# Second projection of the last feed forward by seven products instead of eight

## The reference, cut to what matters

```python
D_MODEL = 1024; SEQ = 512; D_FF_2 = 4 * D_MODEL
# end of second_block, x is [1, 512, 1024]
f = rmsnorm(h, pre_ff_g[l]) @ w_ff1[l]          # [512,1024] @ [1024,4096]
f = jnp.square(jax.nn.relu(f)) @ w_ff2[l]       # [512,4096] @ [4096,1024]
h = h + rmsnorm(f, post_ff_g[l])
```

## Time and profile before

| | before |
|---|---|
| median of 3 runs | 1729.57 us (1729.56 to 1731.13) |
| the profiled execution, own time | 1730.73 us |
| its span, first to last instruction | 1729.0 us |
| mean granted clock of TensorE | 0.998 |
| TensorE busy | 1715.3 us, 99% |
| VectorE busy | 1209.1 us, 70% |
| ScalarE busy | 820.2 us, 47% |
| feed forward of the last block, steady part | about 1440 to 1690 us |

### The profile page before, as it was taken

The page is one execution under the profiler, slowest core; times in us unless marked ns, Lnnn a source line. Parts: engine busy times, 40 slices in busy tenths (PEclk is TensorE's granted clock), DMA queues, the critical chain, the costliest instruction groups (busy, mean ns, idle before and its releaser), DMA issues.

```text
span 1729.0 us, 26320 instructions
## 1 busy us (share of the span) xinstructions
PE 1715.3 (99%) x10458; PEld 1497.2 (87%) x10458; DVE 1209.1 (70%) x1975; ACT 820.2 (47%) x1449; POOL 46.4 (3%) x103
## 2 busy tenths in 40 slices
PE   9999999999999999999999999999999999999998
PEld 8777788999999887777989999989888898999997
DVE  4588787777787735666877777868446876677776
ACT  4477744444445235664444444443565555333342
POOL 0212000000000000000000000000000000000000
PEclk9999999999999999999999999999999999999999
DMA  8343332333334232224133333352314224333331
GB/s 276 113 134 118 119 89 87 109 98 110 101 99 153 86 105 84 81 91 122 39 103 98 110 110 97 99 165 82 110 44 140 63 73 126 106 98 98 100 109 49
DMA packets 220125, 181.36 MB, mean 105 GB/s; under 512 B 9906, under 2 KB 178771, under 8 KB 220003
## 3 DMA queue, kind: packets, MB, share of 16 engines
q1 hardware_dynamic: 217954, 175.48, 33.1%
q0 software_dynamic: 2048, 4.20, 0.9%
HBM read 173.32 MB, written 7.38 MB: 105 GB/s over the span
## 4 chain that ended last, share of the span: by engine, by line
PE 93%; DVE 4%; ACT 1%; DMA 1%; issue 1%; POOL 0%; DVEq 0%; POOLq 0%
PE ps L733 29%; PE ps L734 28%; PE ps L735 28%; PE ps L1092 1%; PE ps L1137 1%; PE ps L1163 1%; PE ps L1112 1%; PE ps L1151 1%; DMA arena<-arena 1%; PE ps L987 1%; DVE wlo L1701 0%; DVE xl L1793 0%; PE ps L1102 0%; PE ps L972 0%; ACT whi L1321 0%
## 5 line engine op out<-in xcount | busy, mean ns | idle before, releaser
L1701 DVE TENSOR_TENSOR wlo<-raw,whi 128x1024 fp32r<-128x1024 f32 (+1 forms) x276 | 317.6, 1167 | 181.3 <-ACT whi L1321 181.0
L733 PE MATMUL ps<-xh,whi 128*128 128x256 f32 (+1 forms) x1016 | 332.4, 327 | 2.3 <-DVE xl L1793 2.3
L735 PE MATMUL ps<-xh,wlo 128*128 128x256 f32 (+1 forms) x1016 | 326.1, 321 | 0.0
L734 PE MATMUL ps<-xl,whi 128*128 128x256 f32 (+1 forms) x1016 | 325.9, 321 | 0.0
L1321 ACT ACTIVATE whi<-raw 128x1024 fp32r<-128x1024 f32 (+1 forms) x276 | 274.6, 1007 | 80.9 <-DMA raw<-in_w_ff 36.4
L733 PE MATMUL ps<-whi,hh 128*128 128x512 f32 x728 | 288.7, 397 | 1.4 <-DVE wlo L1701 1.3
L734 PE MATMUL ps<-wlo,hh 128*128 128x512 f32 x728 | 285.2, 392 | 0.0
L735 PE MATMUL ps<-whi,hl 128*128 128x512 f32 x728 | 283.6, 390 | 0.0
L733 PEld LDWEIGHTS ps<-xh,whi 128*128 128x128 f32 x1016 | 194.1, 191 | 25.8 <-issue 8.8
L735 PEld LDWEIGHTS ps<-xh,wlo 128*128 128x128 f32 x1016 | 194.1, 191 | 14.4
L734 PEld LDWEIGHTS ps<-xl,whi 128*128 128x128 f32 x1016 | 194.4, 191 | 12.2
(11 more groups left out here) (272 smaller groups left out, 2935.3 us busy)
## 6 DMA issues: line engine op xcount, KB each, us to landing
raw<-in_ffn_w_in SPq DMA_DIRECT2D x88, 512.0 KB, 3.8
raw<-in_w_ff SPq DMA_DIRECT2D x64, 512.0 KB, 4.2
raw<-in_ffn_w_out SPq DMA_DIRECT2D x44, 512.0 KB, 3.9
raw<-in_a_w_qkv SPq DMA_DIRECT2D x22, 512.0 KB, 5.5
raw<-in_w_in SPq DMA_DIRECT2D x20, 512.0 KB, 3.8
raw<-in_kv_w SPq DMA_DIRECT2D x16, 512.0 KB, 4.1
bias_skewed<-bias_rows SPq DMA_DIRECT2D x8, 640.0 KB
arena<-arena POOLq DMA_DIRECT2D x64, 64.0 KB, 2.7
```

The source lines that it names most:

```text
L733: e.matmul(o, ah, bh, start=start, stop=False, **more)
L734: e.matmul(o, ah, bl, start=False, stop=False, **more)
L735: return e.matmul(o, al, bh, start=False, stop=stop, **more)
L1701: e.tensor_tensor(lo[:, 0:n], src, f32(hi[:, 0:n]), ALU.subtract).then_inc(s.lo, 1)
```

## The change

Six of the eight groups (`SEVEN_FIRST` 1 to `SEVEN_LAST` 6) are computed by seven products in place of eight. A group's operand is a 2 by 2 matrix of quarters on the left (256 tokens by two hidden blocks: a11, a12, a21, a22) and on the right (two hidden blocks by 512 columns). The seven products are P1 to P7 in the order of the table `SEVEN`: a11, a12, s1, s4, s2, s3, a22. Each has two halves a and b (token tiles), and a half is six matmuls of 512 columns, as a piece was.

- **TensorE** does 14 halves a group instead of 16 pieces. 9548 instructions become 9476.
- **Left operands.** Hidden values are no longer split as they come but kept as fp32 words. VectorE forms the four sums s1, s2, s4, s3 (`left_sum`), ScalarE writes the high part of each of the seven left operands and VectorE the low part (`left`), two products ahead of use.
- **Right operands.** There are seven tiles to split a group instead of four. Four are loads of weights into buffers of `x`. Sums of weight tiles are made by four accumulating transfers a group, each 512 KB from HBM added to the buffer (GpSimd's queue): in one chain the same buffer is split, added to, split again, three times over (P1, P3, P5 and P7 use its states), and another buffer is loaded and added to once (P6).
- **Results.** P1, P2 and P7 add to the left columns: VectorE, six additions a group. P3 to P6 go to the right columns: ScalarE copies each half from PSUM to one of four slots, with its sign, and GpSimd issues a transfer that adds it to `mb` (eight a group, 256 KB each). A bank that a later product goes on adding to is first read out.
- **Order.** "2222" becomes "2212", seven halves for one pair.
- **Around it.** `x` is parked in HBM during the stage and brought back; the gain is loaded late; some semaphores are merged; and all weight tiles, in every stage of the kernel, are laid out on the host so that a tile is 128 rows of 4 KB in HBM.

Counted from P1b, one group's order on TensorE, with the first projection's products between: P2a X6 P2b P3a X4 X3 P3b P4a X5 X1 P4b X7 X2 P5a P5b X6 P6a P6b X4 X3 P7a P7b X5 X1 P1a X7 X2 P1b, 14 X and 14 halves.

```diff
-FEED_PIECES = ["1111"] + ["2222"] * 13
+FEED_PIECES = ["1111"] + ["2212"] * 13
+SEVEN_FIRST, SEVEN_LAST = 1, 6
+SEVEN = [("a11", 0, True, 0, 0, 1), ("a12", 1, True, 0, 0, 1), ("s1", 1, True, 1, 1, -1), ("s4", 1, False, 0, 1, -1),
+         ("s2", 0, False, 0, 1, -1), ("s3", 0, False, 1, 1, -1), ("a22", 0, False, 1, 0, 1)]
...
+    def seven(self, g):
...
+        rights = [Right(a, ("load", landed), [(a, "a", (first, 1))]), Right(b, ("load", b_need), (), b_next),
+                  Right(a, ("a", 48 * turn + 16), [(a, "a", (last, 1))]),
+                  Right(c, ("load", c_need), [(d, "d", (last, 1))], c_next),
+                  Right(a, ("a", 48 * turn + 32), [(a, "a", (last, 0))]), Right(d, ("d", 16 * turn + 16), (), d_next),
+                  Right(a, ("a", 48 * turn + 48), (), following)]
...
+                self.step("seven", piece)
...
+                self.step("seven_post", piece)
+                if t == 1:
+                    self.left(u + 2)
...
# VectorE
+            elif what == "left_sum":
...
+                if name == "s1":
+                    e.tensor_tensor(tmp, a22, a21, ALU.subtract).then_inc(s.left_sum, 1)
...
+            elif what == "seven_post" and not arg[0].nh:
...
+                e.tensor_tensor(self.mb[:, p.tile, 0:512], self.mb[:, p.tile, 0:512], ps[p.bank][:],
+                                ALU.add).then_inc(s.fadd, 1)
+            elif what == "left":
+                u, name, b, entry, _, _ = arg
+                hi, lo = self.left_parts(entry)
+                w.wait_ge(s.left_hi, u + 1)
+                e.tensor_tensor(lo, self.left_source(name, b), f32(hi), ALU.subtract).then_inc(s.left_lo, 1)
# ScalarE
+            elif what == "left":
...
+                e.activation(self.left_parts(entry)[0], self.left_source(name, b), ACT.Copy).then_inc(s.left_hi, 1)
+            elif what == "seven_post" and arg[0].nh:
...
+                e.activation(self.evict_to(p.sent), ps[p.bank][:], ACT.Copy, scale=float(p.sign)).then_inc(s.evicted, 1)
# GpSimd
+            elif what == "split" and self.plan.units[arg[0]][0] == "seven":
...
+                    if chain == "a":
+                        w.wait_ge(s.lo, m + 1)
...
+                    e.dma_start(self.x[:, buffer, :], self.row_tile(*source),
+                                accum_op=ALU.add).then_inc(s.right_sum[chain], 16)
+            elif what == "seven_post" and arg[0].nh:
...
+                e.dma_start(self.mb[:, p.tile, p.nh * 512:p.nh * 512 + 512], self.evict_to(p.sent), accum_op=ALU.add).then_inc(s.added[p.sent % 4], 16)
# SyncE
         def weights(m):
...
+            e.dma_start(self.raw[:, m % RAW, :], ap["c_tiles"][m]).then_inc(s.raw[m % RAW], 16)
```

More of the change, by code:

```diff
@@ L61, in __init__ @@
         self.kind, self.nh, self.t, self.bank, self.i = kind, nh, t, bank, i
-        self.norm, self.group, self.value = norm, group, None
+        self.norm, self.group, self.value, self.added = norm, group, None, None
+class Piece:
+    def __init__(self, u, unit, t, bank, start, before, value, tile, nh, sign, sent, earlier, after):
+        self.u, self.unit, self.t, self.bank, self.start, self.before, self.value = u, unit, t, bank, start, before, value
+        self.tile, self.nh, self.sign, self.sent, self.earlier, self.after = tile, nh, sign, sent, earlier, after
+class Right:
+    def __init__(self, buffer, need, sums=(), load=None):
+        self.buffer, self.need, self.sums, self.load, self.before = buffer, need, sums, load, None
 class Pair:
-    def __init__(self, kind, n, table, columns, blocks):
+    def __init__(self, kind, n, table, columns, blocks, first=None):
         self.kind, self.table, self.columns, self.blocks = kind, table, columns, blocks
@@ L350, in rows @@
                 self.step("rows_post", r)
+                if kind == "f" and group == 0:
+                    self.plain_rows = r.value
             yield
@@ L707, in feed @@
         self.small = [(SPLIT + EXTRA + i, ("t_lo", 12)) for i in range(2)]
-        rows = [self.rows("f", ("w_ff2_2", 0), f0, nf, group=g) for g, (f0, nf) in enumerate(FEED_GROUPS)]
+        self.step("seven_load")
+        self.left(0)
+        rows = [self.rows("f", ("w_ff2_2", 0), f0, nf, group=g) if not SEVEN_FIRST <= g <= SEVEN_LAST else self.seven(g)
+                for g, (f0, nf) in enumerate(FEED_GROUPS)]
         pieces = itertools.chain(*rows[:-1])
-        self.pairs([Pair("relu", f // 2, "w_ff1_2", (f * 128, f * 128 + 128), [f % 8, f % 8 + 1])
+        self.pairs([Pair("relu", f // 2, "w_ff1_2", (f * 128, f * 128 + 128), [f % 8, f % 8 + 1], f)
                     for f in range(FEED_PLAIN, 32, 2)], pieces, FEED_PIECES, AHEAD_FEED, FEED_FIRST)
@@ L1080, in tensor @@
                         "v": (s.v, n), "res": (s.res, n), "mvb": (s.vb, n), "mv": (s.gv, n), "w": (s.mb, n),
-                        "f": (s.fadd, n - 8) if r.group else (s.fb, n)}[r.kind]
+                        "f": (s.fadd, n - 8 + FADD) if r.group else (s.mb, n + 8)}[r.kind]
+            elif what == "seven":
+                p, = arg
+                b, c = p.bank, slice(p.t * 128, p.t * 128 + 128)
+                wh, wl = self.weight(p.unit, 2)
+                lh, ll = self.left_parts(self.plan.entry_of[p.u])
+                w.wait_ge(s.lo, p.unit + 1)
+                w.wait_ge(s.left_lo, p.u + 1)
+                if p.before is None:
+                    w.wait_ge(*freed[b])
+                else:
+                    w.wait_ge(self.events[p.before[0]], p.before[1])
+                for k in (0, 1):
+                    m = mm3(e, ps[b][:], lh[:, k, c], ll[:, k, c], wh[:, k, :], wl[:, k, :], p.start and k == 0, k == 1,
+                            skip_group_check=True)
+                m.then_inc(s.rows, 1)
+                freed[b] = (self.events[p.after[0]], p.after[1])
             elif what == "scores_a":
@@ L1314, in scalar @@
                     w.wait_ge(s.raw[tile % RAW], self.raw_at[tile])
+                elif kind == "seven":
+                    what, value = tile.need
+                    w.wait_ge(s.right[tile.buffer] if what == "load" else s.right_sum[what], value)
                 else:
@@ L1754, in vector @@
                 for i, k in enumerate(pair.blocks):
+                    if pair.kind == "relu":
+                        for n in range(8 * (SEVEN_LAST - SEVEN_FIRST) - 4, 8 * (SEVEN_LAST - SEVEN_FIRST)):
+                            w.wait_ge(s.added[n % 4], 16 * (n // 4 + 1))
                     w.wait_ge(s.hh, pair.hidden[i] + 1)
@@ L2259, in sync @@
                 m, = arg
-                _, _, tile = self.plan.units[m]
+                kind, right, tile = self.plan.units[m]
+                if kind == "seven" and right.load is not None:
+                    w.wait_ge(s.hi, m + 1)
+                    w.wait_ge(s.lo, m + 1)
+                    rows_load(*right.load)
                 if tile is not None and tile + RAW < len(self.plan.tiles):
```

379 lines of the change are left out of this document (280 added, 99 removed).

## The result

| | kernel before | changed kernel |
|---|---|---|
| median of the runs, us | 1729.72 (4 runs) | 1751.03 (1748.96 to 1751.46, 4 runs) |
| span of the profiled execution, us | 1729.0 | 1747.2 |
| TensorE busy / without work, us | 1715.3 / 13.7 | 1710.9 / 36.3 |
| group of four blocks in the steady part, us | 42.08 | 45.46, 44.96, 44.94, 43.40, 44.88 |

Slower: ratio 1.0119, 95% interval [1.0101, 1.0137]. The forecast was 1736.6 us, the range ended at 1751, and slower had a chance of 0.55. The measured median lies on that upper end.

What follows compares the result with a forecast made beforehand. VectorE's and ScalarE's order would set the pace: a group 44.2 us instead of 42.08, +10.6 over five cycles, -2.8 for the sixth group, -0.7 at the head, in all +7.1; forecast 1736.6 us, range 1717 to 1751.

Steps and rivals of the forecast that it cites:

- forced waits: VectorE waits for ScalarE's copy of a left sum, 0.77 us three times; with tiles behind them 3.6 us a group.
- slow transfers (C): Rival: accumulating transfers take 12 us or more and block ScalarE at P5's tile; 6 us a cycle, 1761 us; chance 0.12.
- TensorE's saving: Two pieces fewer a group, 2.76 us; 16.5 us over six groups, 72 matmuls.
- The work of VectorE and ScalarE: Per group, VectorE rises from 30.3 to 36.8 us and ScalarE from 16.0 to 24.7, against TensorE's 39.3.
- Legs 1 to 3: VectorE to P6's low half, 24.2 us; TensorE and ScalarE to 30.1; VectorE to P7a's sum, 37.4.
- the walk: Following three engines through one cycle from P1b's end to the next: 43.1 us a group if right operands are in time.
- Leg 4: Cycle's last stretch on TensorE: P1a, X7, X2, P1b take 5.6 us, ending the cycle at 43.1.
- The transfers: Accumulating transfers take 7.0 us; up to 5.9 is hidden, so they add 1.1 us a cycle, making 44.2.
- rival B: Accumulating transfers are as quick as a load and stay hidden; +1.5 us, 1731 us; chance 0.18.
- Five cycles: Five full cycles between first group's P1b and last one's, each 44.2 us instead of 42.08: +10.6 us.
- The sixth group, head and tail: Two pieces really saved where VectorE has room, -2.8 us, and a sooner load at the head, -0.7 us.
- Rival A: TensorE keeps the bound, with a period of 39.3 us; 1713 us, or 1721 if half is kept; chance 0.25.

Runs made afterwards that it cites:

- experiment 6: Experiment 5's kernel with ScalarE's high-half copies of the last plain pairs moved behind the next half's read-out; 1728.42 us, ratio 0.9988.
- Experiment 2: Changed kernel with each left sum formed one half earlier than the left parts that use it; 1733.29 us, ratio 1.0018.
- experiment 1: Changed kernel with seven dummy matmuls filling TensorE's gap ahead of P1a in groups 2 to 6; 1744.37 us, ratio 1.0085.
- experiment 4: Changed kernel with both kinds of accumulating transfer made plain copies of the same size on the same queue; 1749.25 us, ratio 1.0107.
- experiment 5: Changed kernel with left sums one half earlier and first-projection weight sums right before the split that uses them; 1729.01 us, ratio 0.9993.
- experiment 3: Changed kernel with the first projection's four weight sums moved right before the split that uses them; 1741.42 us, ratio 1.0067.
- experiment 7: Experiment 6's kernel with two of the four left sums of a group (s1 and s3) given to GpSimd; 1729.09 us, ratio 0.9991.

## Why the prediction was right, and where its sizes were off

Right in sign and in the main mechanism, the forced waits; 14 us too low. That it lies in the range at all is partly luck. The forecast gave its own mechanism 1733 to 1746 us, and 1751.03 lies above that, on the very end of the range, where the prediction had put slow transfers (C), which did not come. One sign of being right failed too, narrowly: VectorE was to be busy for 85% or more, and it was busy for 83% of the group shown (37.17 of 44.96 us).

- **TensorE's saving**: 16.5 us forecast. In experiment 6, where the clock fell nowhere in the cycles, TensorE was busy for 1700.9 us, 14.4 less than before. By starts, another 1.5 us are matmuls at the lower clock in its tail.
- **The work of VectorE and ScalarE**: 36.8 and 24.7 us forecast, 37.2 and 24.1 measured.
- **The forced waits** were there at the three places, 0.70 us each, and so were the tiles behind them. Experiment 2 shows them to be the largest single cause. It moved four sums and changed no amount of work, and it took 17.7 of the 21.3 us away, in five groups 10 us by the order and 5 by the clock that stayed up with it.
- **Legs 1 to 3** came out at 24.2, 30.2 and 37.6 us (24.2, 30.1 and 37.4 forecast). I did not name the gap at P3a (0.76 us), because in the walk VectorE's leg covered it; the walk's end came out without it. Two times in the walk don't follow from its terms: eight halves at 1.38 and eight products at 1.43 are 22.5 us, not 22.9, and leg 2's terms end at 29.9, not 30.1. Leg 1's end is VectorE's and doesn't hang on the first; the second moves the cycle by 0.2 us at most. Whether it helps to bring the clock down was not tried by itself.
- **Leg 4 is the step that failed**: "P1a, X7, X2, P1b, 2 x 1.38 + 2 x 1.43 = 5.6". It took P's and X's time at full clock, and the granted clock fell behind the gap that leg 3 makes. To the end of P1b it was 7.4 us. With the gap filled (experiment 1) the group is 43.4 us, so this was 1.6 us for each of the groups it struck. In the whole stage matmuls at the lower clock make up 9.4 us, head and tail included.
- **The transfers** were sized at 7.0 us and cost 1.1 us a cycle in the sum. They took 5.7, under the room of 5.9, and cost nothing, as rival B had it; experiment 4 agrees. The rule of the Trainium skill that I weighed gave 4.4 us as an estimate (DMA: Bandwidth & Descriptors, "Anatomy of one DMA — SWDGE (gpsimd) path", with the two source reads of Collectives: The Full Stack, "The bandwidth ceiling: the fold count and why AG ≠ RS ≠ AR", which speaks of reductions between cores). The trace has 5.7 against it, and agrees with it only in that the transfer is hidden.
- **Five cycles**: +10.6 forecast and +13.2 measured (223.64 - 210.4). Without the transfers' 5.5, and with 1.6 for each of the five times that the clock fell in these groups (the first has it twice, behind 2.41 and 1.83 us), it would have been +5.1 + 8.0 = 13.1: two errors that nearly cancel, which is luck.
- **The sixth group, head and tail**: -3.5 forecast, +5.0 measured (18.2 - 13.2). "The tail, where VectorE has room" was wrong: TensorE stands still there for 6.0 us in five gaps; three of them, 4.9 us with the longest of 2.91, are waits for ScalarE's read-outs. Experiments 5 and 6 show the order's part and that something else lies right behind it. The additions in the transfers cost about 0.9 us there (experiment 4). What the head has of the 5.0 was not worked out.
- **Rival A** (TensorE keeps the bound) did not hold in any version: the steady group is 40.5 us at best, 1.2 above 39.3. **Rival C** did not come about.

The medians differ by 21.3 us and the spans by 18.2. The other 3.1 us have no row: the profiled execution of the changed kernel was the quickest of its four, 2.1 us below their median, with a mean granted clock of 0.994 against 0.992 in the others, and that of the kernel before was 1.0 us above its own.

## What to carry to other kernels

Where a helper engine goes to nine tenths of the pace of the main one, count its order and not its sum: a pair "sum, then the part that needs another engine's copy of it" costs the hand-over each time. Forming the sums one half earlier removed 17.7 us here without removing any work, about a third of it because the clock stayed up. Price a new gap of the main engine by its length and by what the clock does behind it. And look at the place where the pattern ends: here the engines' orders no longer fitted each other there, and TensorE lost 4.9 us on waits that the forecast had at 0.

## What the runs showed of the hardware

- TensorE's clock fell to its lower level 0.3 to 1.5 us after the restart behind a gap, and stayed there for about 3.4 us. The length of the gap doesn't decide it. Behind 1.83 us, with gaps of 0.76 and 0.69 us earlier in the cycle, it fell four times in five (changed kernel) and three times in five (experiment 4); behind 1.83 us alone once in five (experiment 2); behind 2.00 us three times in five (experiment 3). In the steady cycles gaps of up to 1.54 us left it up (experiment 5), but so did one of 2.42 us at the head of experiment 4 and one of 3.18 us in the tail of experiment 7. Needless matmuls in the gap kept it up too, and made the kernel 6.7 us faster.
- An accumulating transfer landed after 5.7 us where the same transfer as a copy took 4.2 (512 KB from HBM), and after 6.1 where the copy took 3.1 (256 KB, on-chip to on-chip), both on GpSimd's queue.
- A 128x512 subtraction on GpSimd (s3) doubled the time of the 128x1024 subtraction that VectorE began 0.05 us behind it, 1.22 to 2.68 us. Where VectorE's began 0.2 us ahead of GpSimd's s1, VectorE's kept its 1.22 us and s1 took 2.15 us, where it had taken 1.29 and 1.68 in the first two groups (experiment 7).
- A gap of TensorE costs more than the idle time that the trace shows: 0.37 us of idle at P6a put the rest of the cycle 0.62 to 0.64 us back (experiment 7 against 6). By starts, 0.16 of it is that the idle time counts from the shown end of the last matmul, 0.39 us long, where the next would have begun 0.23 after its start; and the first matmul behind a gap takes 0.31 to 0.34 us to the next start, not 0.23.
